# Cached sample keys scored during the input projection, one-pass norm spreads, alternating sample heads

## The reference

```python
h = rmsnorm(x); proj = h @ w_in          # (tokens x 1024) @ (1024 x 2828)
# group A: gated, 31-tap depthwise convolution, layernorm, silu
# group B: 4-tap convolution and silu on q, k, v, then the gated delta rule
cb = silu(causal_dwconv(qkv_b)); q, k = l2norm(q), l2norm(k)
o_d, new_s = gated_delta_rule(q, k, v, g, beta, s_delta)
# group C: attention with a forget gate; a sample attends to 8 cached pages of 128 tokens and to itself
s = einsum('bqhd,bkhd->bhqk', q, k_all) * scale + (decay terms)
o_f = softmax(s) @ v_all
# for each sample and head of group B: one step of the recurrence on a 64 x 64 state
S = a * (I - b * k k^T) S + b * k v^T;   o = S^T q / 8
```

## Time and profile before

| what | value |
|---|---|
| time, median of 3 runs | 1725.76 us (1724.69 to 1727.97) |
| the profiled execution: its own time | 1725.11 us |
| its span in the trace | 1723.5 us |
| mean granted TensorE clock | 0.953 of full speed |
| busy: PE, DVE, ACT, POOL | 94 %, 47 %, 24 %, 12 % |
| projection, delta rule, samples | about 316, 195 and 104 us |
| prompt attention, mixing and feed-forward | 136 and 906 us |

### The profile page before, as it was taken

One profiled execution on the slowest core, in us unless ns is written; L12 is line 12 of the kernel. 1 busy time (PEld: TensorE's weight loads), 2 busy tenths in 40 slices (PEclk: granted clock), 3 DMA queues, 4 the chain that ended last, 5 costly groups with the idle time before them and its releaser, 6 DMA issues.

```text
span 1723.5 us, 32325 instructions
## 1 busy us (share of the span) xinstructions
PE 1612.6 (94%) x13775; PEld 1484.1 (86%) x13775; DVE 814.2 (47%) x1426; ACT 414.0 (24%) x707; POOL 204.3 (12%) x261
## 2 busy tenths in 40 slices
PE   7999999987998797898899999999999999999995
PEld 6899987886888584665787999999999999999995
DVE  6359766417887222555565242342432433423426
ACT  5323221222222101545554211111101111111102
POOL 4242000007553000111001000000000000000003
PEclk9999999989999656999899999999999999999998
DMA  6031111103221310411622111111011111111122
GB/s 195 23 96 40 37 38 51 49 23 102 76 77 40 95 19 27 120 42 35 231 77 85 37 50 62 37 49 62 25 50 55 34 59 37 50 62 37 37 98 100
DMA packets 112065, 108.70 MB, mean 63 GB/s; under 512 B 15330, under 2 KB 101805, under 8 KB 111906
## 3 DMA queue, kind: packets, MB, share of 16 engines
q1 hardware_dynamic: 108146, 103.86, 19.3%
q0 software_dynamic: 3776, 2.77, 0.9%
HBM read 93.98 MB, written 12.93 MB: 62 GB/s over the span
## 4 chain that ended last, share of the span: by engine, by line
PE 46%; DVE 3%; ACT 2%; issue 0%; DMA 0%; DVEq 0%
PE mf_ps L2550 28%; PE mf_ps L2557 14%; PE mf_ps L2510 3%; PE mf_ps L2538 1%; DVE h_lo L2388 1%; ACT h_hi L2299 1%; ACT mo_buf L196 0%; DVE mo_buf L2449 0%; DVE ff_scaled L2421 0%; DVE mo_x L2453 0%; ACT mo_buf L2344 0%; PE mf_ps L2578 0%; DMA mo_o_raw<-in_w_out_dram 0%; PE mf_ps L2520 0%; DVE ff_w_lo L2395 0%
## 5 line engine op out<-in xcount | busy, mean ns | idle before, releaser
L2414 DVE TENSOR_TENSOR ff_acc<-ff_acc,mf_ps 128x344 f32<-128x344 f32 x264 | 135.2, 513 | 186.8 <-PE mf_ps L2557 186.6
L2550 PE MATMUL mf_ps<-h_lo,ff_w_hi 128*128 128x344 f32 x1008 | 213.8, 320 | 0.0
L2550 PE MATMUL mf_ps<-h_hi,ff_w_hi 128*128 128x344 f32 x1008 | 213.6, 320 | 0.0
L2550 PE MATMUL mf_ps<-h_hi,ff_w_lo 128*128 128x344 f32 x1008 | 212.7, 319 | 0.0
L2557 PE MATMUL mf_ps<-ff_h_hi,ff_d_hi 128*128 128x344 f32 x528 | 169.8, 322 | 3.7 <-DVE ff_h_lo L2409 3.7
L2557 PE MATMUL mf_ps<-ff_h_hi,ff_d_lo 128*128 128x344 f32 x528 | 169.7, 321 | 0.0
L2550 PEld LDWEIGHTS mf_ps<-h_hi,ff_w_lo 128*128 128x128 f32 x1008 | 169.2, 188 | 0.0
L2550 PEld LDWEIGHTS mf_ps<-h_hi,ff_w_hi 128*128 128x128 f32 x1008 | 169.1, 188 | 0.0
L2557 PE MATMUL mf_ps<-ff_h_lo,ff_d_hi 128*128 128x344 f32 x528 | 168.9, 320 | 0.0
L2550 PEld LDWEIGHTS mf_ps<-h_lo,ff_w_hi 128*128 128x128 f32 x1008 | 168.8, 188 | 0.0
L747 PE MATMUL pc_main<-h_hi,in_whi 128*128 128x344 f32 x528 | 120.1, 337 | 1.6 <-PEq L91 1.6
(11 more groups left out here) (437 smaller groups left out, 2564.8 us busy)
## 6 DMA issues: line engine op xcount, KB each, us to landing
fs_keys<-in_cache_k_dram SPq DMA_DIRECT2D x64, 192.0 KB, 2.5
fs_values<-in_cache_v_dram SPq DMA_DIRECT2D x64, 192.0 KB, 2.5
in_raw<-in_w_in_dram SPq DMA_DIRECT2D x22, 512.0 KB, 3.9
ff_raw<-in_w_gate_dram SPq DMA_DIRECT2D x22, 512.0 KB, 3.9
ff_raw<-in_w_up_dram SPq DMA_DIRECT2D x22, 512.0 KB, 4.1
ff_d_raw<-in_w_down_dram SPq DMA_DIRECT2D x22, 512.0 KB, 5.5
ld_x<-in_x_prompt_dram SPq DMA_DIRECT2D x8, 512.0 KB, 4.5
mo_o_raw<-in_w_out_dram SPq DMA_DIRECT2D x8, 512.0 KB, 8.1
```

Of the source, the lines that this page charges most:

```text
L2414: dve.tensor_tensor(part, part, ps[:, b, 0:TG], ALU.add).then_inc(down_added, 1)
L2550: last = pe.matmul(bank(t % 2 * 3 + g)[:, 0:TG], a[:, k], b[:, k, group(g)], start=(k == 0 and n == 0), stop=(k == KD - 1 and n == 2))
```

## The change

1. **Order of tiles.** The three tiles of the attention's queries come right after the four of group A (places 4 to 6); the convolved tiles take 7 to 15, the attention's keys 16 to 18, the last three stay. The scaled query rows of the 8 samples go to the chip's memory and each sequence's row is broadcast back to 128 partitions by DMA.
2. **Keys scored here.** 64 cached pages come one by one into three buffers: SP loads page n when page n-3 was reduced, POOL multiplies it by the query row (128x384), DVE reduces it to 128x6. Three pages in each of DVE's steps 9 to 16, then 6, 6, 9, 9 and 10 in steps 17 to 21. The delta rule loses its key loads, PE's spread of the query, ACT's copy of it and DVE's 24 products and 24 reductions.
3. **One-pass spreads.** The row of inverse norms is cut into a high and a low part on 12 + 12 rows of one operand (ACT copies the high part, DVE's `lower_inverse` the low), so that one matmul of the one-pass number format does what two passes did. Sums and spreads go by 9 pieces of 128 tokens, not 12 of 86. The spreads now stand in tiles 16 to 18.
4. **Queues.** ACT instead of SP issues the weights' DMA; ACT instead of POOL issues the stores of keys and convolution rows. DVE writes the gated values of group A where the 31-tap convolution reads them, which drops two copies on ACT (L775).
5. **Samples.** The two halves e alternate within each pair of sequence and head; there is one signal at the end of the stream and not one after each half.

```diff
-        order = list(range(T_Z)) + [T_KC + j ...] + [T_QC + j ...] + [T_Z + j ...]
+        order = list(range(T_QB)) + [T_QC + j for j in range(PAIRS)] + list(range(T_QB, T_Z)) + [
+            T_KC + j for j in range(PAIRS)] + [T_Z + j for j in range(PAIRS)]
...
-            at_slot, at_k = (14, 2 + n) if n < 6 else (15, n - 6) if n < 14 else (16, n - 14)
+            at_slot, at_k = (16, 4 + n) if n < 4 else (17, n - 4) if n < 12 else (18, (n - 12) // 2)
...
+        scored_in = {s: range(3 * (s - 9), 3 * (s - 8)) for s in range(9, 17)}
+        scored_in.update({17: range(24, 30), 18: range(30, 36), 19: range(36, 45), 20: range(45, 54), 21: range(54, 64)})
...
+                def load_page(n):            # SP
+                    b, g = page_of[n]
+                    if g == 0:
+                        if b >= 2:
+                            sp.wait_ge(page_used, NPAGE * (b - 1))
+                        sp.dma_start(q_rows[b % 2][:], q_dram[b:b + 1].to_broadcast([P, DW])).then_inc(q_in[b % 2], 16)
+                    if n >= 3:
+                        sp.wait_ge(page_scored, n - 2)
+                    page = sp.value_load(m.pages[0:1, n:n + 1], min_val=0, max_val=NPHYS - 1)
+                    sp.dma_start(pages[n % 3][:], ...).then_inc(page_in[n % 3], 16)
+                def multiply_page(n):        # POOL
+                    pool.wait_ge(page_in[n % 3], 16 * (n // 3 + 1))
+                    pool.tensor_tensor(pages[n % 3][:], pages[n % 3][:], q_rows[b % 2][:], ALU.mult).then_inc(page_used, 1)
+                def score(n):                # DVE
+                    dve.wait_ge(page_used, n + 1)
+                    dve.tensor_reduce(m.fs_s[:, b, g], pages[n % 3][:] ..., AX_X, ALU.add).then_inc(page_scored, 1)
...
-                        wait_emptied(pe, number["inv", g])
-                        last = pe.matmul(bank[:, 0:TG], m.head_rows[:, j], inv_rows[:, group(g)], start=True, stop=True)
+                        wait_emptied(pe, number["inv", NG - 1])
+                        last = pe.matmul(bank[:, 0:TG], m.head_hl[:, j], inv_hl[:, group(g)], start=True, stop=True)
...                                          # samples, PE
-                for e in range(2):
-                    for b in range(NS):
-                        for i in range(PAIRS):
+                for b in range(NS):
+                    for i in range(PAIRS):
+                        for e in range(2):
                             pe.matmul(seq_banks(e)[half(e), b, i], ... value row ...)
+                        for e in range(2):
                             last = pe.matmul(seq_banks(e)[half(e), b, i], ... keys, state ...)
```

More of the change, by code:

```diff
@@ L516, in project_and_convolve @@
         sb_rows = at("pc_sb_rows", [NS * (KB - 1), 3 * DW], F32, offset=of_tile(T_KC))
+        b_rows = at("pc_b_rows", [KB - 1 + NS, 3 * DW], F32, offset=of_tile(T_KC))
+        inv_hl = at("pc_inv_hl", [32 + 2 * H, T], F32R, offset=of_tile(T_KC + 2))
+        in_a = Place(of_tile(T_A), of_tile(T_GATE))
+        sa = in_a("sa", [P, 2, NS, KA - 1])
+        later = in_a("later", [P, NS, NPAGE, H])
+        in_a = Place(of_tile(T_A), of_tile(T_GATE))
+        q_rows = [in_a(f"q_rows{s}", [P, DW]) for s in range(2)]
+        pages = [in_a(f"page{s}", [P, DW]) for s in range(3)]
         gap = Place(ring.end, O_FOX)
@@ L677, in fill @@
                         pe.wait_ge(squared, j + 1)
-                        for c in range(NT):
-                            last = pe.matmul(bank[0:TT, 2 * c:2 * c + 2], sq[j % 2][:, c * TT:(c + 1) * TT],
+                        for c in range(CHUNKS):
+                            last = pe.matmul(bank[:, 2 * c:2 * c + 2], sq[j % 2][:, chunk(c)],
                                              m.head_ones[:, 0:P:HD], start=True, stop=True)
@@ L712, in fill @@
                             pe.wait_ge(a_squared, j + 1)
-                            for c in range(NT):
-                                last = pe.matmul(bank[0:TT, c:c + 1], sq_a[:, j, c * TT:(c + 1) * TT], m.ones[:, 0:1],
+                            for c in range(CHUNKS):
+                                last = pe.matmul(bank[:, c:c + 1], sq_a[:, j, chunk(c)], m.ones[:, 0:1],
                                                  start=(j == 0 and c == 0), stop=(j == 1), skip_group_check=True)
@@ L870, in _ @@
-                    if s == 18:
+                        conv_rows(0)
+                    if s == 15:
+                        act.wait_ge(zeroed, 2)
+                        for g in range(NG):
+                            bank, n = empty("inv", g), 512 if g < 2 else NS
+                            act.copy(inv_hl[0:2 * H, g * 512:g * 512 + n], bank[0:2 * H, (0 if g < 2 else P - NS):][
+                                :, 0:n]).then_inc(inv_hi, 1)
+                        conv_rows(1)
+                    if s == 16:
+                        conv_rows(2)
+                        wait_emptied(act, number["b_rows", 2])
+                        act.dma_start(m.o_conv_b_p[0, 0], b_rows[0:KB - 1]).then_inc(b_stored, 16)
+                        act.dma_start(m.o_conv_b_s[0, :, KB - 2], b_rows[KB - 1:KB - 1 + NS]).then_inc(b_stored, 16)
@@ L1661, in _ @@
                             top_spread, 1)
+                last.then_inc(x_ready, 1)
                 for i in range(PAIRS):
```

398 lines of the change are left out of this document (190 added, 208 removed).

## The result

The changed kernel takes 1706.74 us (median of 4 runs, 1705.97 to 1707.25) where the kernel before takes 1725.91: a ratio of 0.9887, with a 95 % interval of 0.9871 to 0.9904. It is faster by 19 us, 28 us slower than the forecast of 1679.1, and above the range (1658 to 1703). The profiled execution took 1706.5 us, with a span of 1704.8.

What follows compares the result with a forecast made beforehand. PE was taken to bound the projection (busy 307.2 of 312.5 us) and to do slow work at low clock in the samples. 1725.1 + 4 (projection) - 17 (delta rule) - 33 (samples) = 1679.1 us, range 1658 to 1703.

Steps and rivals of the forecast that it cites:

- PE's own work in the projection: Projection: one-pass spreads, smaller sums and a lost stall at the mean take 16 us (12 to 20) from PE.
- The stalls: Projection: side pieces on PE wait for DVE behind long work in several places, +19 us (+5 to +30).
- `b_rows`: Projection: its last piece waits for the first spread to be multiplied in, behind step 16's scores and taps, +4.8 us.
- `a_spread`: Projection, step 20: this side piece on PE stands behind nine pages on DVE, 3.4 us.
- The tail: End of the projection: the last pages fit beside PE and ACT, so DVE ends the phase only 1 us later.
- The delta rule: Without scoring, DVE readies PE's operands sooner: 1.9 us per chunk for 8 chunks plus 2, -17 us (-10 to -22).
- The samples: Alternating halves overlap weight loads: stream -27 us, query product -5, maxima's spread -1, in all -33.
- (1): Samples: value rows share rows and do not overlap, 96 records keep 200 ns, 13.4 us later, 1692.5 us; chance 0.14.
- (2): Projection: POOL's products block DVE's taps and cuts, eight convolution steps 2 to 2.5 us longer, 1697 us; chance 0.14.
- (3): Projection: the pages' round trip takes 8.5 us, 2.8 a page, and PE stops with DVE, +50, 1729 us; chance 0.05.
- (4): Samples: the denser stream brings the clock up to 2.4 GHz, 1667 us; chance 0.12.
- (5): Delta rule: the change buys only L1534, as PE's dependences through ACT take over, -6, so 1690 us; chance 0.10.

Runs made afterwards that it cites:

- values-first stream: The changed kernel with all 48 value matmuls of the samples' stream before all 48 state matmuls: 1696.21 us, 0.9839 to the kernel before.
- the unscored kernel: The kernel before with the cached keys' scoring taken out of the delta rule and put nowhere: 1706.42 us, 0.9889 to the kernel before.

## Why the prediction was wrong

**PE's own work in the projection: too large.** The forecast took 16 us off. 12.8 of them were 18 spreads at 0.71; measured are 18 x 0.42 = 7.6, since one matmul between others of the main stream costs 0.54 and I had put 0.25: 0.16 for its 344 columns and 0.09 for a switch around it, which came from no row. The rows beside L758 above suggest that the excess belongs to the change from 128 rows to 44 and back; no run varies that. `sums` gave back nothing: 12.4 us of busy time for 108 passes, where 144 took 11.6.

**The stalls: right in their places and in their sum.** +19 with their dips was forecast. Measured are 11.7 us of waits (16.7 for 5.0), and by the windows' clock (0.95 of 323 us, 0.97 of 312.5) up to 7 us more lost at the low level. That the sum came out is in part luck: `b_rows` waited 1.5 us where 4.8 were put, `a_spread` 5.0 where 3.4 were. With these, PE ends 10.8 us later than before, for +3 forecast. Most of the difference is the work: about 8 us went, not 16.

**The tail: with the samples' stream, the step that failed most.** Each missed by 7.7 us. "The phase ends +1 later by DVE's tail" is 8.7 us in the trace: 13.1 from PE's end to the next phase for 4.4. 3.3 of them are DVE behind ACT. A page took 1.6 us there, as forecast; but PE and ACT were quicker over the last tile than the pages. 5.1 are POOL's DRAIN, which I had not looked for: it stands in neither sum nor rivals. In the trace of before, POOL's DRAIN is over 43 us before the barrier opens, so its length could cost nothing, and the change made POOL one of the last to finish.

**The delta rule: right in place and size.** Forecast -17; measured -2.0 a chunk by the period, and -18.4 by the unscored kernel. In the changed kernel 4 us of this are lost to the clock, 17.8 us at 0.50 for some 6 before. The prediction had no term for how long the clock stays low at the start of a phase. The idle time in front would not have given one, as the table above shows.

**The samples: right in what overlaps, wrong in what holds a record.** "So a record is not held by its 64 columns, but by the load of weights after the one before in the same place." The values-first stream takes 54 ns a record, so this was not the whole of it: in a stream that changes between 8 rows and 64 rows at each group, a group takes 0.41 us whether two records stand in it or four. That is 48 x 0.41 = 19.7 of the stream's 20.1 us. The rows of before bear this out just as well as my reading, for there every group of two changes too: 96 x 0.40 = 38.4. I took the delta rule's pace from a stretch in which no row count changes, and did not ask what else was different.

**The rivals.** (1), value rows without overlap: they overlap in full, so the earlier trace rows were read rightly, and the Trainium skill's "TensorE: Matmul & The Clock Gate", Part 3, "The mechanism", is not borne out in this case: the halves of value rows share their 8 rows, and four records take the time of two. (2), POOL's products holding DVE: the products and the taps of the changed kernel, with minimum, median and maximum in ns:

```profile
L655 POOL TENSOR_TENSOR pc_page<-pc_page,pc_q_rows x64: 991/1011/2147, 175.4 to 394.2; 128x384 f32<-128x384 f32 x64
```

```profile
L954 DVE SCALAR_TENSOR_TENSOR proj<-pc_pad,cols_a,proj x60: 1272/1280/2046, 109.4 to 296.3; 128x1024 f32<-128x1024 f32 x60
```

Laid side by side, 9 of the 64 products met a tap in time. They took 1.80 us in the mean, the other 55 took 1.02 (one of them 1.81, beside a cut of weights); of the 60 taps one took 2.05 us and the rest 1.27 to 1.29. In eight of the nine meetings the product waited, in the ninth the tap. So the two do shut each other out, as the Trainium skill's "SBUF — State Buffer", "SBUF: two separate sides", says (the trace agrees: the five slowest, 2.0 to 2.1 us, are products after nearly a whole tap), but the one that waits is nearly always POOL, which has time. DVE lost under a microsecond: the pages land in DVE's convolution, which reads PSUM, and in its reductions. (3), the round trip: 1.6 us a page and not 2.8; it decides nothing by its pace, but 40 pages in five tiles left no slack, which the version with pages earlier shows (8.5 us). (4) didn't come: the clock stays at 0.50 through the stream. (5) fell with the delta rule's -18.4.

## What to carry to other kernels

A barrier waits for the slowest engine's drain, not for the last row of the timeline. Before moving work to an engine that used to finish early, find out how long its drain takes, and let it end that much sooner, or take its transfers from it. Where small matmuls are slow, count the changes of shape between neighbours before the records themselves: overlapping the halves brought the stream from 39.0 to 20.1 us, and grouping like with like brought it from there to 10.9. And work that is hidden behind waits on other engines is only hidden if nothing behind it in the same queue is waited for.

## What the runs showed of the hardware

- GpSimd's DRAIN at the end of a phase took 6.6 to 7.9 us in phases in which GpSimd had issued transfers, even when the last was 200 us old, and 1.1 when SyncE issued the same ones.
- In a stream that changed between matmuls of 8 rows and of 64 rows at each group, a group took 0.40 to 0.41 us at 1.2 GHz with two records or four; without changes four records took 0.21. That the row count is what counts is the best reading, not a proof.
- A product on GpSimd and a tap on VectorE, both with two operands in SBUF, held each other up at each of their nine meetings: eight products took 1.27 to 2.15 us for 1.02, one tap 2.05 for 1.28.
- Two float32 matmuls on the same 8 rows and different column halves ran at the same time: they started 7 ns apart.
- The clock stayed at 0.50 for the first 5.3 to 6.2 us of the delta rule after 10.9 to 16.4 us of idle time in three versions, and for 15.0 to 17.5 after 4.5 to 5.4 us in two others: the length of the idle time didn't set it.
